# Fillers for TensorE at the start and at the end of the delta rule in a two-layer streaming encoder step

## The reference

```python
def step(S, xs):
    qc, kc, uc, wc, gcc, ac = xs
    v_new = uc - jnp.einsum('bhck,bhkv->bhcv', wc, S)
    o = (jnp.einsum('bhck,bhkv->bhcv', qc * jnp.exp(gcc)[..., None], S)
         + jnp.einsum('bhij,bhjv->bhiv', ac, v_new))
    g_last = gcc[..., -1]
    S = (S * jnp.exp(g_last)[..., None, None]
         + jnp.einsum('bhck,bhcv->bhkv', kc * jnp.exp(g_last[..., None] - gcc)[..., None], v_new))
    return S, o
```

## Time and profile before

| | us |
|---|---|
| median of 3 runs | 1714.24 |
| lowest, highest run | 1710.45, 1722.09 |
| profiled execution, its time | 1710.72 |
| profiled execution, its span | 1709.0 |
| TensorE busy with matmuls in the span | 1635.6 (96%) |
| TensorE busy with weight loads | 1554.6 (91%) |
| VectorE, ScalarE, GpSimd busy | 747.8, 602.7, 533.2 |
| mean granted clock of TensorE | 0.983 of full speed |

### The profile page before, as it was taken

One profiled execution on the slowest core, in us unless ns is written; L12 is line 12 of the kernel. 1 busy time (PEld: TensorE's weight loads), 2 busy tenths in 40 slices (PEclk: granted clock), 3 DMA queues, 4 the chain that ended last, 5 costly groups with the idle time before them and its releaser, 6 DMA issues.

```text
span 1709.0 us, 31660 instructions
## 1 busy us (share of the span) xinstructions
PE 1635.6 (96%) x13441; PEld 1554.6 (91%) x13441; DVE 747.8 (44%) x1338; ACT 602.7 (35%) x1105; POOL 533.2 (31%) x192
## 2 busy tenths in 40 slices
PE   6999998999999999999999998999899999999998
PEld 6999977898988899999999995569888999999998
DVE  4593056434645522323225416765755323222245
ACT  5122254223435422313133317764444313222232
POOL 3633201121441343343434331003522433334341
PEclk9998999998999999999999999899999999999999
DMA  5231211004240222222222241002411232222321
GB/s 154 75 98 52 75 52 57 2 2 136 93 130 26 75 92 82 98 76 98 76 96 91 82 150 37 1 1 75 148 50 50 75 99 80 95 92 80 98 74 53
DMA packets 123034, 131.39 MB, mean 77 GB/s; under 512 B 6285, under 2 KB 115122, under 8 KB 122930
## 3 DMA queue, kind: packets, MB, share of 16 engines
q1 hardware_dynamic: 116064, 123.27, 22.3%
q10 hardware_dynamic: 6866, 6.63, 1.2%
HBM read 122.44 MB, written 7.45 MB: 76 GB/s over the span
## 4 chain that ended last, share of the span: by engine, by line
issue 42%; PE 42%; POOL 8%; DVE 4%; ACT 2%; DMA 1%; ACTq 0%; POOLq 0%; DVEq 0%
PE LP L744 34%; POOL wl L638 8%; PE LP L1101 2%; DVE acc L1865 1%; PE MP L882 1%; PE LP L833 1%; DVE xl L1872 1%; DMA stage<-in_w_in_ab 1%; PE MP L856 0%; DVE conv_sum L2022 0%; DMA stage<-in_w_xkv 0%; PE MP L945 0%; ACT sq L1381 0%; PE MP L873 0%; PE MP L1101 0%
## 5 line engine op out<-in xcount | busy, mean ns | idle before, releaser
L638 POOL TENSOR_TENSOR wl<-stage,wh 128x2048 fp32r<-128x2048 f32 x107 | 493.4, 4611 | 989.4 <-ACT wh L1356 989.3
L744 PE MATMUL LP<-xh,wh 128*128 128x272 f32 x2176 | 457.3, 291 | 15.3 <-DVE xl L1872 8.1
L744 PE MATMUL LP<-xh,wl 128*128 128x272 f32 x2176 | 452.1, 289 | 0.0
L744 PE MATMUL LP<-xl,wh 128*128 128x272 f32 x2176 | 450.8, 289 | 0.0
L1356 ACT CAST wh<-stage 128x2048 fp32r<-128x2048 f32 x107 | 203.8, 1906 | 459.0 <-PE LP L744 458.1
L744 PEld LDWEIGHTS LP<-xh,wh 128*128 128x128 f32 x2176 | 344.5, 190 | 20.4 <-DVE xl L1872 10.7
L744 PEld LDWEIGHTS LP<-xl,wh 128*128 128x128 f32 x2176 | 344.2, 190 | 0.0
L744 PEld LDWEIGHTS LP<-xh,wl 128*128 128x128 f32 x2176 | 341.8, 190 | 0.0
L744 PE MATMUL LP<-hh,wh 128*128 128x272 f32 x1024 | 211.2, 287 | 0.0
L744 PE MATMUL LP<-hh,wl 128*128 128x272 f32 x1024 | 210.5, 288 | 0.0
L744 PE MATMUL LP<-hl,wh 128*128 128x272 f32 x1024 | 210.4, 287 | 0.0
(11 more groups left out here) (378 smaller groups left out, 1809.1 us busy)
## 6 DMA issues: line engine op xcount, KB each, us to landing
stage<-in_w_up SPq DMA_DIRECT2D x32, 1024.0 KB, 5.4
stage<-in_w_down SPq DMA_DIRECT2D x32, 1024.0 KB, 5.2
stage<-in_w_in_ab SPq DMA_DIRECT2D x13, 1024.0 KB, 5.2
stage<-in_w_xkv SPq DMA_DIRECT2D x8, 1024.0 KB, 5.3
stage<-in_w_in_c SPq DMA_DIRECT2D x6, 1024.0 KB, 5.1
stage<-in_w_out_ab SPq DMA_DIRECT2D x4, 1024.0 KB, 9.4
stage<-in_w_xq SPq DMA_DIRECT2D x4, 1024.0 KB, 5.3
stage<-in_w_xo SPq DMA_DIRECT2D x4, 1024.0 KB, 5.7
```

Source lines behind the costliest of these rows:

```text
L638: pool.tensor_tensor(wl[s][:, :], stage[s][:, :], wh[s][:, :].bitcast(f32), ALU.subtract).then_inc(w_lo, 1)
L744: mm = pe.matmul(LP[:, 2 * slot + half, 0:b - a], weights, X[part][:, k, a:b], start=(first and n_ == 0), stop=(last and n_ == 2), skip_gr ...
```

## The change

Four places get fillers, twelve before the first turns, two in each of the first five steps of the first product, and two before `ws` and two before `ds` in the last three chunks (q = 6, 7, 8). As the fillers of the delta rule write to bank 0 of `MP`, a wait for the last turn to be read back stands ahead of the first of them. Nothing is removed or moved, and no other engine's list changes.

```diff
             pe.wait_ge(mask_done, FIRST_MASKS)
+            keep_busy(12, LP[:, 3, :])
             pe.wait_ge(par_loaded, 16 * 8)
...
             def first_reads(i):
                 if i + 3 < KT:
                     turn_x(i + 3)
+                if i < 5:
+                    keep_busy(2, LP[:, 3, :])
                 pe.wait_ge(xs_ready, i + 1)
...
                         if j < TT:
                             pe.wait_ge(turn_used, TURNS.index(("w", j)) + 1)
+                    if q >= 6:
+                        pe.wait_ge(turn_used, len(TURNS))
+                        keep_busy(2, MP[:, 0, :])
                     if q:
                         pe.wait_ge(rec_dve, 2 * q)
...
                 elif name == "ds":
+                    if q >= 6:
+                        keep_busy(2, MP[:, 0, :])
                     pe.wait_ge(rec_dve, 2 * q + 1)
```

## The result

The changed kernel takes 1727.06 us (median of 11 runs, 1718.14 to 1734.71); the kernel before, run beside it, 1713.31 us (11 runs, 1710.45 to 1733.37). The ratio is 1.0063, 95% interval 1.0038 to 1.0088: slower by 0.6%, some 14 us by the medians, where 3.5 us faster was forecast. The time lies outside the range of 1704 to 1717, on the wrong side.

What follows compares the result with a forecast made beforehand. TensorE, nine tenths busy, was taken as the bound, with time to win where it idles or runs at half clock. A gain of 2.8 us plus 0.7 for earlier falls gave 1714.24 - 3.5 = 1710.7 us, range 1704 to 1717.

Steps and rivals of the forecast that it cites:

- The change, part by part: Prediction section pricing each filler group by TensorE time: a filler pair 0.45 us at full clock, 0.87 at half.
- The twelve ahead of the first turns: At the start, 5.2 us of fillers inside TensorE's wait for rows until 10.55: price 0, gain 0.
- The pairs of the first five steps: First product: fillers fit idle time, dense stretch still starts at 31.22; price 0, at most 0.4 us, gain 0.
- The pairs before ws and ds: Last three delta-rule chunks: ws pairs cost 0.15 us, mostly in idle time; ds pairs lie on the chain, 1.2 us.
- What they give back: Last chunk at full clock saves 3.03 us; with a faster output product, head sums come 2.8 us earlier.
- The gain against the median: Whole kernel: 2.8 us plus 0.7 for earlier clock falls gives 3.5, so 1714.24 becomes 1710.7 us.
- The term for an earlier fall: Delta rule: each further slow chunk costs 2.2 us, which fillers would also win; 0.7 us taken on average.
- the clock falls all the same: Rival, last chunks: fillers cost 1.8 us and half clock still comes in 376 to 391; 1716.0 us, chance 0.13.
- The start pays: Rival, start: in slower executions TensorE wakes late and fillers repair it, 1.5 us more; 1709.2 us, chance 0.06.
- Nothing of it is on the path: Rival, delta rule: ds pairs hide behind vnew when GpSimd's subtract slows VectorE; gain 4.5, 1709.7 us, chance 0.06.
- the fall only moves: Rival: a new clock fall at head sums or attention gives back 2 to 3 us; 1713.5 us, chance 0.15.

Runs made afterwards that it cites:

- padded kernel: The changed kernel with all its fillers plus 80 long-satisfied waits (40 instructions) ahead of the first filler; ratio to before 0.9950, median 1710.27 us.
- ten tiny matmuls: The kernel before with 10 matmuls of 32 x 32 added ahead of the first turns (39 instructions), no real fillers; ratio to before 1.0012.
- The two controls: The kernel before with 10 (39 instructions) or 44 (shift of 175) tiny 32 x 32 matmuls and no real fillers; ratios to before 1.0012 and 0.9997.

## Why the prediction was wrong

**The step that failed** is the pricing in "The change, part by part": each filler was priced by the time for which it holds the engine, and where a wait covers it, at 0 ("Price 0" for the twelve and for the pairs of the first steps). There is no term for what 135 more instructions do to the place of everything behind them, and none of the rivals has it. The row for it was on the page, 78 instruction packets, and the profile of the kernel before shows two thirds of the MLP loop running without one. Had I asked how near to its limit that loop is, 6.1 blocks would have told that about one position in ten (26 of 256) is a bad one for each of the two loops, and that a shift by 135 of a start at about 104 lands there. That term is +17 us in the profile, against a sum of -2.8. The ratios agree: without the stall the same fillers have 0.9950, 17 us are 1.0%, and 1.0063 was measured.

**The twelve ahead of the first turns**: right. They ran from 2.01 us on and ended at 6.6, earlier than forecast, since the clock rose on the way, and 3.13 us of the wait for DMA remained:

```profile
2.01 4.62 PE L819 MATMUL LP<-ident 128*128 128x128 f32 x24 [2.01 <-POOL ident L642]
9.76 0.46 PE L905 MATMUL MP<-ident,par_rows 121*128 121x121 f32 x1 [3.13 <-DMA conv_rows<-in_state_gdn_conv]
...
11.39 3.67 PE L918 MATMUL MP<-ident,x_rows 128*128 128x128 f32 x16
```

The transposes behind them take 3.67 us, exactly as before. The clock had been up and fell again in the pause (granted 0.50 from 10.0 to 15.3 us), so these twelve bought nothing. Had there been no pause, the gain would still be 0, as forecast. In the padded kernel the fillers ran up to the rows' arrival and the transposes were 1.5 us shorter, but the product's first step then waited 3.36 us for xl and began at 16.82, only 0.13 earlier than in the changed kernel:

```profile
5.40 4.47 PE L819 MATMUL LP<-ident 128*128 128x128 f32 x24 [5.40 <-issue]
...
10.85 2.17 PE L920 MATMUL MP<-ident,x_rows 128*128 128x128 f32 x16
...
16.82 0.82 PE L744 MATMUL LP<-xh,wh 128*128 128x272 f32 x2 [3.36 <-DVE xl L1882]
```

The same page of the Trainium skill as in the prediction (TensorE: Matmul & The Clock Gate, "Why this matters for your kernels") warns of such idle gaps between bursts, and here the trace agrees (the gap was 3.13 us).

**The pairs of the first five steps**: right. The dense stretch begins at 30.82 instead of 31.22, and the cast of the first weights, which is ahead of VectorE's whole chain, 0.39 earlier as well (12.76 against 13.15), by its DMA. The rest of the difference is nil.

**The pairs before ws and ds**: right in kind. Forecast 0.15 and 1.2 us, measured about 0 and 1.48: each ds pair is fully on the chain, at 0.49 and not 0.4. Their sum, 1.35 forecast, is 1.33 by the three chunks: 14.60 against 4.37 + 4.30 + 4.60, where 4.60 is the prediction's 4.56 for a last chunk at full clock and 0.04 to the product's start.

**What they give back**: right. The last chunk ran at 1.00, from its ws to the product in 5.00 us instead of 7.63, and the first four steps of the product, up to the head sums, took 3.73 us (395.58 to 399.31) instead of 4.45. From the ws of q = 6 to the head sums that is 18.33 us instead of 20.75, a gain of 2.4 where 2.8 was forecast. That both stand later in the profile after than before is due to falls of the clock between 270 and 340 us that this execution had and the profiled one of before hadn't; the execution with ten tiny matmuls, which has no fillers at the delta rule, shows them too.

One profile can't tell whether fillers hold the clock, but the fourteen together do. Times from the ws of q = 6, this profile's among them:

| delta rule's fillers | profiles | to the output product, us | to the head sums, us |
|---|---|---|---|
| both pairs | 8 | 14.60 in each | 18.3 in six, 19.8 and 20.0 in two |
| pairs before ws only | 1 | 13.13 | 16.86 |
| none | 5 | 16.29, 16.31, 18.18, 22.03, 22.15 | 20.76, 20.75, 23.78, 27.63, 27.69 |

With fillers the granted clock is 1.00 through the three chunks in all nine. Without them it falls in all five: in the last chunk alone in two (the profile of before is one), in q = 6 in the other three.

**The gain against the median**, forecast at 3.5 us, was too small, as soon as the stall is out of the way: five measurements of four versions with the delta rule's fillers and something at the start give ratios from 0.9927 to 0.9964, that is 6 to 13 us, and the fillers alone 0.9973 and 1.0001. The two controls have 1.0012 and 0.9997. The profile of the kernel before was one of the fastest executions. In the five without fillers at the delta rule the head sums come 24.1 us after the ws of q = 6 on average, against 18.3: 5.8 us, where 2.8 and 0.7 were forecast. The term for an earlier fall was too small: a chunk that is slow from its start takes 7.2 us (385.29 to 392.50 with ten tiny matmuls), 2.9 more than at full clock and not 2.2. The rest of the 6 to 13 us isn't traced to a place.

**The rivals**: "the clock falls all the same" forecast a slower time too, 1716.0, but by a fall in the last chunks, and that didn't take place in any profile with fillers. The loss has the sign of this rival and nothing of its mechanism or size. "The start pays" found no support: with real fillers at the start or tiny matmuls in their place the ratios are alike (0.9950 and 0.9964, 0.9958 and 0.9927). "Nothing of it is on the path" is refuted by the 1.48 us. Whether "the fall only moves" holds in part the profiles don't settle, since the falls outside the delta rule differ from one to the next.

## What to carry to other kernels

Instructions that an engine issues while it waits anyway are not free: they move all code behind them. In front of a long loop (6.1 blocks of instructions here), find out (from the instruction packets and the waits for "issue" at the jumps back) whether it is still held and how far its start is from a place where it isn't, and count a change in instructions as well as in microseconds. Before a small edit is believed or thrown away for a few us, pad the program by some tens of instructions and time it again. Of the versions run, the changed kernel without the pairs ahead of ds, or with 40 instructions of padding, is faster than both kernels.

## What the runs showed of the hardware

- Two TensorE loops of 1563 instructions run with no load of instructions at most positions, and load all their instructions in each round at others. The first jump back then costs 4.07 to 4.08 + 0.82 to 1.11 us of stall in layer 0's loop and 3.85 + 1.92 us in layer 1's, and the half clock behind it some 3 to 4 us more in layer 0's; both together are about 8.5 us a jump.
- An instruction packet (16384 bytes) that arrives during the store of the two states goes with a store of 3.3 to 3.5 us instead of 1.95 to 1.97 (three profiles against eleven).
- In the last three chunks of the delta rule the clock falls in five of five profiles without fillers, and stays at 1.00 in nine of nine with them. In the profile of before it falls with no pause over 0.5 us ahead of it.
- The same kernel, unchanged, scatters by 20 us from execution to execution (1709.5 to 1730.3 us in 29 runs), and its median is 1713.3, 1721.2, 1715.5 and 1722.5 us in four sets. The mean granted clock goes with it: 0.983 in the run of 1709.5 us, 0.969 in the one of 1730.3. The padded kernel scatters less (1706.8 to 1716.0 us in 12 runs), the one with the delta rule's fillers alone hardly (1707.4 to 1730.4 in 12).
- Fillers in front of a pause didn't keep the clock over it: 24 full matmul records up to 6.6 us, and half clock again by 10 us. Without a pause they did: in the padded kernel they ran up to 9.87 us, and the 16 transposes behind them took 2.17 us instead of 3.67.
